# The last output job with tokens standing, and the last LayerNorm done token tile by token tile from PSUM

## The chip, the cores and the metric

The kernel runs on one core of a Trainium2 chip. The metric is the device time of one execution in microseconds (us). TensorE (PE in the rows) does matrix products and transposes into PSUM, VectorE (DVE) and ScalarE (ACT) work on SBUF and PSUM, GpSimd (POOL) works on SBUF, and SyncE (SP) issues the DMAs.

## The reference, cut to what matters

Two models run one behind the other on 512 tokens with 1024 channels. The part that this change touches is the very end of the second: the sum of the residual and the output projection, and the LayerNorm over the channels, whose result is the kernel's output.

```python
def layer_norm(x, g, b):
    xf = x.astype(jnp.float32)
    mu = xf.mean(-1, keepdims=True)
    var = jnp.square(xf - mu).mean(-1, keepdims=True)
    return ((xf - mu) * lax.rsqrt(var + LN_EPS) * g.astype(jnp.float32) + b.astype(jnp.float32)).astype(x.dtype)

def second_block(...):
    ...
        y = jnp.concatenate([y_mix, y_mem], axis=-1) * jax.nn.silu(gate)   # 512 x 2048
        x = layer_norm(ALPHA * x + y @ w_out, pg, pb)                      # w_out: 2048 x 1024
    return x
```

## The kernel before

All products are float32 products of some precision: each operand is split into a high part and a low part (`x_hi`, `x_lo`, `w_hi`, `w_lo`, type fp32r), and three products are summed, hi by hi, hi by lo and lo by hi. The weights come in *jobs* of 256 output columns and 8 blocks of 128 rows. SP loads the weights of a job into `w_raw`, GpSimd splits them (L738 and L751), TensorE multiplies. Two sets of weights and two pairs of PSUM banks (`g_bank` 0 and 1 for even jobs, 2 and 3 for odd ones) are used in turn. A semaphore `w_used` tells that a job's products are done, `g_free` that its banks were read.

Everything but the attention is kept transposed, with channels on the 128 partitions and the 512 tokens in the free dimension: the residual is `hT`, eight chunks of 128 channels by 512 tokens. A job in `products_T` (L888) holds the weights still and moves the tokens: for each of two halves of 128 output channels 8 times 3 matmuls of 512 columns, so 48 in all. Other jobs (`products_nat`, L915) hold a tile of 128 tokens still and move the weights: 24 matmuls of 256 columns for each of the tiles, and the result has tokens on the partitions.

The last projection (`b_out`) is 8 jobs: four with the first half of the 2048 rows, four with the second. After each, VectorE adds the two banks to two chunks of `hT` (L2731 in `add_out`). The last three jobs and the LayerNorm are interleaved, before the change, in `last_output_jobs` on TensorE and in `layer_norm` on VectorE and ScalarE:

- after job 5 TensorE multiplies chunks 0 and 1 by a matrix of ones (L1385), which gives a first estimate of the mean in every partition; VectorE takes it off the chunks (L2774, `centre`), ScalarE squares them (L2070), VectorE sums chunks and squares in PSUM (L2781, `add_up`), all beside jobs 6 and 7;
- after job 7 come the last chunk (L2807, L2774, L2070), the sums over the partitions with the ones (L1395 to L1399), the mean (L1526), the variance (L2822), its transpose to one value per token (L1406), the root (L2077) and the reciprocal (L2828);
- VectorE (L2816) and GpSimd with ScalarE (L856, L1526) take the rest of the mean off and multiply by the gain; TensorE transposes 32 blocks of 128 by 128 to have tokens on the partitions (L1519); VectorE (L2979), or ScalarE and GpSimd (L1526, L869), multiply by the reciprocal root and add the bias row; SP writes eight tiles of 128 by 512 to HBM (L707).

The order of the work is the order of the code on each engine; nothing reorders it. `plan_banks` assigns the four banks of `t_bank` to the transposes and sums in turn. `link` and `done` on VectorE make an instruction signal its own semaphore and make the next one wait for it; `done` also adds one empty instruction for each further semaphore.

## Time and profile before

| what | us |
|---|---|
| median of 3 runs (1693.11 to 1694.98) | 1694.58 |
| the profiled execution's own time | 1694.56 |
| its span in the profile | 1692.8 |
| TensorE busy | 1663.4 (98%) |
| VectorE busy | 916.9 (54%) |
| ScalarE busy | 572.4 (34%) |
| GpSimd busy | 1053.0 (62%) |

The page of the profile lists busy time by engine, the span in 40 slices, the chain of work that ended last, and the costliest groups of instructions. A row of the timeline or of the chain gives start and length in microseconds; `x4` means that four instructions in a row were merged, with the length from the first one's start to the last one's end. The length of a matmul contains its way through the array, so matmuls that follow each other overlap in the rows: the pace is the distance of two starts. TensorE is busy to its last slice but one tenth; in the last of the 40 slices (42 us long) it is busy for 7 tenths.

### The profile page before, as it was taken

The numbers are of one execution on the slowest core, as the hardware profiler recorded it, in microseconds if no ns is written. First come the engines' busy times: TensorE is split into PE (matmuls) and PEld (weight loads), VectorE is DVE, ScalarE is ACT, GpSimd is POOL, SyncE is SP. The second block draws the span as 40 slices with busy tenths as digits, with TensorE's granted clock in tenths as the row PEclk, the third lists the DMA queues.
The fourth block names the chain that finished last, engine by engine and source line by source line (L and its number), as shares of the span: only waits on it lengthen the run. The fifth ranks groups of instructions, "written<-read, shape, count | busy, mean of one in ns | idle before, by whom it ended". The sixth has DMA issues, their size and how long they took to land.

```text
span 1692.8 us, 22289 instructions
## 1 busy us (share of the span) xinstructions
PE 1663.4 (98%) x8073; PEld 1364.6 (81%) x8073; DVE 916.9 (54%) x1411; ACT 572.4 (34%) x990; POOL 1053.0 (62%) x779
## 2 busy tenths in 40 slices
PE   7999999999999999999999999999999999999997
PEld 5897997888878888888888888887878777777785
DVE  5323948782445222221247997998475784443416
ACT  5331248330422100100144445756131345553203
POOL 7676754476647766766774889782577544333563
PEclk9999999999999999999999999999999999999999
DMA  6333333223343323333233332221423321121221
GB/s 207 125 102 121 104 100 125 96 79 100 100 149 94 92 93 95 99 100 100 81 117 101 99 100 90 77 83 54 162 72 106 95 75 51 51 74 51 75 87 50
DMA packets 191274, 162.10 MB, mean 96 GB/s; under 512 B 9684, under 2 KB 187472, under 8 KB 190672
## 3 DMA queue, kind: packets, MB, share of 16 engines
q1 hardware_dynamic: 190984, 160.84, 30.5%
q8 instruction: 56, 0.92, 0.2%
q14 instruction: 34, 0.28, 0.0%
q10 hardware_dynamic: 200, 0.06, 0.0%
HBM read 155.60 MB, written 4.23 MB: 94 GB/s over the span
## 4 chain that ended last, share of the span: by engine, by line
PE 92%; DVE 4%; ACT 2%; POOL 1%; issue 1%; DMA 0%; DVEq 0%; SPq 0%; ACTq 0%
PE g_bank L888 65%; PE g_bank L905 7%; PE g_bank L915 6%; PE t_bank L1465 2%; PE t_bank L1475 2%; PE g_bank L1369 1%; PE t_bank L1205 1%; PE t_bank L1237 1%; PE t_bank L1287 1%; PE t_bank L1308 1%; PE g_bank L1351 1%; PE t_bank L1454 1%; PE t_bank L949 1%; PE t_bank L1445 1%; DVE t_bank L2647 0%
## 5 line engine op out<-in xcount | busy, mean ns | idle before, releaser
L751 POOL TENSOR_TENSOR w_lo<-w_raw,w_hi 128x512 fp32r<-128x512 f32 x392 | 541.1, 1411 | 8.2
L738 POOL TENSOR_SCALAR w_hi<-w_raw 128x2048 fp32r<-128x2048 f32 x98 | 192.6, 1965 | 497.4 <-issue 214.0
L888 PE MATMUL g_bank<-x_hi,w_hi 128*128 128x512 f32 x1248 | 494.8, 396 | 0.2 <-DVEq L2222 0.2
L888 PE MATMUL g_bank<-x_hi,w_lo 128*128 128x512 f32 x1248 | 486.0, 389 | 0.0
L888 PE MATMUL g_bank<-x_lo,w_hi 128*128 128x512 f32 x1248 | 486.0, 389 | 0.0
L888 PEld LDWEIGHTS g_bank<-x_hi,w_hi 128*128 128x128 f32 x1248 | 234.4, 188 | 52.1 <-issue 4.4
L888 PEld LDWEIGHTS g_bank<-x_hi,w_lo 128*128 128x128 f32 x1248 | 234.3, 188 | 49.2
L888 PEld LDWEIGHTS g_bank<-x_lo,w_hi 128*128 128x128 f32 x1248 | 234.5, 188 | 48.5 <-issue 1.7
L2647 DVE SCALAR_TENSOR_TENSOR t_bank<-hc,cols,t_bank 128x512 f32<-128x512 f32 x280 | 187.0, 749 | 4.7 <-DVE hc L2631 2.8
L799 POOL TENSOR_TENSOR w_lo<-w_raw,w_hi 128x512 fp32r<-128x512 f32 x104 | 134.3, 1324 | 68.1 <-ACT w_hi L1868 68.1
L888 PE MATMUL g_bank<-y_hi,w_hi 128*128 128x512 f32 x332 | 130.9, 394 | 0.0
L888 PE MATMUL g_bank<-y_hi,w_lo 128*128 128x512 f32 x332 | 129.4, 390 | 0.0
L888 PE MATMUL g_bank<-y_lo,w_hi 128*128 128x512 f32 x332 | 129.3, 389 | 0.0
L1859 ACT ACTIVATE sg<-gs 128x512 f32<-128x512 f32 x22 | 14.0, 634 | 253.4 <-DVE gs L2598 253.4
L2598 DVE TENSOR_TENSOR gs<-g_bank,rstd 128x512 f32<-128x512 f32 x22 | 15.2, 691 | 139.9 <-PE g_bank L888 139.6
L888 PEld LDWEIGHTS g_bank<-y_hi,w_hi 128*128 128x128 f32 x332 | 62.3, 188 | 14.2 <-issue 0.7
L888 PEld LDWEIGHTS g_bank<-y_hi,w_lo 128*128 128x128 f32 x332 | 62.3, 188 | 13.2
L888 PEld LDWEIGHTS g_bank<-y_lo,w_hi 128*128 128x128 f32 x332 | 62.4, 188 | 12.8 <-issue 0.2
L815 POOL TENSOR_TENSOR pacc<-pacc,prod 128x512 f32<-128x512 f32 x54 | 68.1, 1293 | 0.0
L2907 DVE CUSTOM_DVE_ANT_0 pB<-t_bank,mask 128x128 f32<-128x128 f32 (+3 forms) x48 | 23.6, 491 | 75.1 <-PE t_bank L1465 68.0
L2251 DVE TENSOR_TENSOR hT<-hT,g_bank 128x512 f32<-128x512 f32 x24 | 15.4, 683 | 84.7 <-PE g_bank L888 67.8
L2731 DVE SCALAR_TENSOR_TENSOR hT<-hT,g_bank 128x512 f32<-128x512 f32 x28 | 18.0, 682 | 74.9 <-PE g_bank L888 54.6
(458 smaller groups left out, 2907.3 us busy)
## 6 DMA issues: line engine op xcount, KB each, us to landing
w_raw<-w_gate_up SPq DMA_DIRECT2D x44, 512.0 KB, 5.0
w_raw<-a_w_in SPq DMA_DIRECT2D x44, 512.0 KB, 4.5
w_raw<-b_w_in SPq DMA_DIRECT2D x38, 512.0 KB, 4.3
w_raw<-w_in SPq DMA_DIRECT2D x28, 512.0 KB, 4.8
w_raw<-w_kv SPq DMA_DIRECT2D x16, 512.0 KB, 4.4
w_raw<-w_out_mix SPq DMA_DIRECT2D x16, 512.0 KB, 6.3
w_raw<-w_down SPq DMA_DIRECT2D x16, 512.0 KB, 3.9
w_raw<-a_w_out SPq DMA_DIRECT2D x16, 512.0 KB, 4.0
```

The source lines that it names most:

```text
L738: nc.gpsimd.tensor_scalar(w_hi[:, par], w_raw[:, par], 1.0, 0.0, ALU.mult, ALU.add).then_inc(pool_chain, 1)
L751: last = nc.gpsimd.tensor_tensor(w_lo[:, par, s], w_raw[:, par, s], w_hi[:, par, s].bitcast(F32), ALU.subtract)
L799: last = nc.gpsimd.tensor_tensor(w_lo[:, par, s], w_raw[:, par, s], w_hi[:, par, s].bitcast(F32), ALU.subtract)
L815: nc.gpsimd.tensor_tensor(acc_k[:], acc_k[:], p[:], ALU.add).then_inc(tap_chain, 1)
L888: last = nc.tensor.matmul(g_bank[:, 2 * pair + f, 0:n], ww[:, k0 + k, ws], xk, start=(k == 0 and q == 0), stop=(k == kt - 1 and q == 2))
L905: last = nc.tensor.matmul(g_bank[:, 2 * par + f, :], ww[:, par, k, ws], xx[:, k0 + k, :], start=(k == 0 and q == 0), stop=(k == kt - 1 and ...
L915: last = nc.tensor.matmul(g_bank[:, 2 * par + m // 2, m % 2 * WC:m % 2 * WC + n], xx[:, k, m * P:(m + 1) * P], ww[:, k, 0:n], start=(k == ...
L1465: last = nc.tensor.matmul(b[:, c:c + W_OF[qb]], qB[:, 4 * hg + i, qb * P:(qb + 1) * P], kB[:, 0:W_OF[qb]], start=True, stop=True)
L1475: last = nc.tensor.matmul(b, vB[:, kt, :], pTB[:, pT_at(u) + kt, :], start=(kt == 0), stop=(kt == qb))
L2647: ins = v.scalar_tensor_tensor(tail if k == TAPS - 1 else a(k), h(k), wk, a(k), ALU.mult, ALU.add)
L2731: ins = v.scalar_tensor_tensor(hT[:, k, :], hT[:, k, :], 1.0 if half else ALPHA, g_bank[:, 2 * (j % 2) + f, :], ALU.mult, ALU.add)
L2907: ins = v.tensor_tensor_reduce(p_unit(u, i), b[:, i % per * W_OF[1]:i % per * W_OF[1] + w], mask[:, M_AT[qb]:M_AT[qb] + w], SLOPES[4 * hg ...
```

## The change

The LayerNorm of layer `b` no longer uses the transposed form. `last_output_jobs` and `layer_norm` serve layer `a` only; what they did for layer `b` is replaced:

- TensorE: no product with ones after job 5. Job 6 signals its first half (`w_half`). Then the finished chunks 0 to 3 of `hT` are transposed, 16 blocks, one bank of `t_bank` for each tile of 128 tokens (task `h_out`). Job 7 is computed with tokens standing: for each of the four token tiles two transposes of chunks 4 and 5 into the first half of a bank of `g_bank`, then 24 matmuls of 256 columns into the second half, and between them two matmuls with `ident` that add chunks 6 and 7 into the same accumulation. Bank `H_BANK[m]` then holds the finished residual of channels 512 to 1023 for tile m, bank `h_out` m that of channels 0 to 511; `h_tok` tells it.
- VectorE: for each tile statistics of both banks (`bn_stats`, `bn_aggr`), then (h - mean) * gain for both halves into `onat`, with the reciprocal of the root between them. For the last tile VectorE also multiplies by the reciprocal root and adds the bias.
- ScalarE: the root for each tile, and for tiles 0 to 2 the product with the reciprocal root in place. GpSimd: the bias for tiles 0 to 2.
- SP: one more row of 1024 values is spread over the partitions (`g_row`, the gain), and the eight output tiles are written in the order of the token tiles.

```diff
-            last_output_jobs(JOBS["b_out"], "b", 1)
-            for i in range(8):
-                h, m = i // 4, i % 4
-                pe.wait_ge(fin_dve, (4, GAIN_DVE)[h])
-                if h:
-                    pe.wait_ge(fin_act, DT - GAIN_DVE)
-                b = bank(TASKS["out"] + i)
-                for q in range(4):
-                    last = nc.tensor.transpose(b[:, q * P:(q + 1) * P], hT[:, 4 * h + q, m * P:(m + 1) * P], ident[:])
+            base = JOBS["b_out"]
+            jobs(base + 5, 1, lambda par: products_T(par, x_hi, x_lo))
+            jobs(base + 6, 1, lambda par: products_T(par, x_hi, x_lo, half=w_half))
+            h0 = 48 + 16 + 8
+            for m in range(TT):
+                b = bank(TASKS["h_out"] + m)
+                pe.wait_ge(h_done, h0 + 4)
+                for k in range(4):
+                    last = nc.tensor.transpose(b[:, k * P:(k + 1) * P], hT[:, k, m * P:(m + 1) * P], ident[:])
                 last.then_inc(t_ready, 1)
+            j = base + 7
+            slot(j, j % 2, j // 2)
+            for m in range(TT):
+                ms = slice(m * P, (m + 1) * P)
+                if m == 2:
+                    pe.wait_ge(g_free[(j + 1) % 2], (j + 1) // 2)
+                b = g_bank[:, H_BANK[m], :]
+                for k in range(4, 6):
+                    pe.wait_ge(h_done, h0 + k + 1)
+                    nc.tensor.transpose(b[:, (k - 4) * P:(k - 3) * P], hT[:, k, ms], ident[:])
+                for k in range(KT):
+                    for q, (xx, ww) in enumerate(((x_hi, w_hi), (x_hi, w_lo), (x_lo, w_hi))):
+                        last = nc.tensor.matmul(b[:, WC:2 * WC], xx[:, k, ms], ww[:, j % 2, k, :],
+                                                start=(k == 0 and q == 0), stop=(k == KT - 1 and q == 2))
+                    if k in (0, 1):
+                        nc.tensor.matmul(b[:, WC + k * P:WC + (k + 1) * P], hT[:, 6 + k, ms], ident[:], start=False, stop=False)
+                last.then_inc(h_tok, 1)
...
@@ ScalarE
-            layer_norm("b", 1, True)
-            act.wait_ge(root_tok, 3)
-            for i in OUT_BY_ACT:
...
+            link(nc.scalar.activation(ltok[:, 0, 0:1], eps[:, 1:2], ACT.Sqrt))
+            def token_std(m):
+                act.wait_ge(tok_var, m + 1)
+                nc.scalar.activation(ltok[:, 1, m:m + 1], tvar[:, m, 1:2], ACT.Sqrt, bias=eps[:, 1:2]).then_inc(ln_std, 1)
+            token_std(0)
+            for m in range(TT - 1):
+                act.wait_ge(root_tok, 2 + m + 1)
+                for i in (2 * m, 2 * m + 1):
+                    copy(onat[:, i, :], onat[:, i, :], ltok[:, 2, m:m + 1]).then_inc(on_act, 1)
+                token_std(m + 1)
...
@@ VectorE
-            layer_norm("b", 1, col["b_post_g"], col["b_post_b"], True)
...
+            j = JOBS["b_out"] + 6
+            dve.wait_ge(w_half, 7)
+            v.tensor_tensor(hT[:, 4, :], hT[:, 4, :], g_bank[:, 2 * (j % 2), :], ALU.add).then_inc(h_done, 1)
+            dve.wait_ge(w_used, j + 1)
+            done(v.tensor_tensor(hT[:, 5, :], hT[:, 5, :], g_bank[:, 2 * (j % 2) + 1, :], ALU.add), h_done, g_free[j % 2])
+            dve.wait_ge(in_brow, 32)
+            for m in range(TT):
+                first = ready(TASKS["h_out"] + m)
+                v.bn_stats(out=tstat[:, m, 0, :], in_=first)
+                dve.wait_ge(h_tok, m + 1)
+                both = (first, g_bank[:, H_BANK[m], :])
+                link(v.bn_stats(out=tstat[:, m, 1, :], in_=both[1]))
+                done(v.bn_aggr(out=tvar[:, m, :], in_=tstat[:, m, :, :]), tok_var)
+                for h in range(2):
+                    ins = v.scalar_tensor_tensor(onat[:, 2 * m + h, :], both[h], tvar[:, m, 0:1], g_row[:, h * T:(h + 1) * T],
+                                                 ALU.subtract, ALU.mult)
+                    if h == 0:
+                        link(ins)
+                        dve.wait_ge(ln_std, 1 + m + 1)
+                        link(v.reciprocal(ltok[:, 2, m:m + 1], ltok[:, 1, m:m + 1]))
+                    elif m < TT - 1:
+                        done(ins, root_tok)
+                    else:
+                        link(ins)
+            for h in range(2):
+                i = 2 * (TT - 1) + h
+                v.scalar_tensor_tensor(onat[:, i, :], onat[:, i, :], ltok[:, 2, TT - 1:TT], b_row[:, h * T:(h + 1) * T],
+                                       ALU.mult, ALU.add).then_inc(on_dve, 1)
...
@@ GpSimd
-            less_rest_of_mean(1)
-            pool.wait_ge(in_brow, 16)
-            for n, i in enumerate(OUT_BY_ACT):
...
+            pool.wait_ge(in_brow, 32)
+            for i in range(2 * (TT - 1)):
+                pool.wait_ge(on_act, i + 1)
+                nc.gpsimd.tensor_tensor(onat[:, i, :], onat[:, i, :], b_row[:, i % 2 * T:(i % 2 + 1) * T], ALU.add).then_inc(on_pool, 1)
```

On TensorE, behind the last matmul of job 7, this stood at the end of the program before (each row an instruction with its line, what it writes and reads, and the semaphores it waits for; `ones` and `ident` are constant matrices, `ln_s` and `nring` the sums):

```order
L888 MATMUL g_bank<-x_hi,w_lo 128x512
L1395 MATMUL t_bank<-ln_s,ones 128x512 [waits ln_sums,t_free0,t_free2]
L1395 MATMUL t_bank<-ln_s,ones 128x512 [waits ln_sums]
L1397 MATMUL t_bank<-hT,ones 128x512 [waits ln_cent]
L1399 MATMUL t_bank<-nring,ones 128x512 [waits ln_sq]
L1406 MATMUL t_bank<-ident,rstd 128x128 [waits ln_var,t_free1]
L1406 MATMUL t_bank<-ident,rstd 128x128 x3
L1519 MATMUL t_bank<-ident,hT 128x128 [waits t_free3,fin_dve]
L1519 MATMUL t_bank<-ident,hT 128x128 x3
```

In the changed program this stands on TensorE from the end of job 6 on:

```order
L884 MATMUL g_bank<-x_hi,w_lo 128x512
L1510 MATMUL t_bank<-ident,hT 128x128 [waits h_done,t_free3]
L1510 MATMUL t_bank<-ident,hT 128x128 x3
...
L1521 MATMUL g_bank<-ident,hT 128x128 [waits h_done,g_free1,w_split]
L1521 MATMUL g_bank<-ident,hT 128x128 [waits h_done]
L1524 MATMUL g_bank<-w_hi,x_hi 128x256
L1524 MATMUL g_bank<-w_lo,x_hi 128x256
L1524 MATMUL g_bank<-w_hi,x_lo 128x256
L1527 MATMUL g_bank<-ident,hT 128x128
```

The 32 transposes behind the LayerNorm (L1519) became 16 ahead of job 7 (L1510) and 8 within it (L1521), with 8 products with `ident` (L1527) for the last two chunks; behind the last matmul of job 7 TensorE has nothing left to do, and within job 7 it waits for VectorE only for chunks 4 and 5 and, at tile 2, for the banks of job 6.

On VectorE this stood in the last stretch before (`hg` is the chunk times the gain, `gneg` the gain over -1024, `ltok` values per token):

```order
L2807 SCALAR_TENSOR_TENSOR hT<-hT,g_bank 128x512 [waits dve_chain,w_used]
L2774 SCALAR_TENSOR_TENSOR hT<-t_bank,hT 128x512 [waits dve_chain,t_ready]
L2816 SCALAR_TENSOR_TENSOR hT<-t_bank,gneg,hg 128x512 [waits ln_cent,hg_ready,ln_d,t_ready]
L2822 SCALAR_TENSOR_TENSOR rstd<-t_bank,rstd 128x512 [waits dve_chain,t_ready,ln_dd]
L2816 SCALAR_TENSOR_TENSOR hT<-t_bank,gneg,hg 128x512 [waits dve_chain,hg_ready] x2
L2828 RECIPROCAL ltok<-ltok 128x4 [waits dve_chain,ln_std]
L2816 SCALAR_TENSOR_TENSOR hT<-t_bank,gneg,hg 128x512 [waits dve_chain,hg_ready] x2
L2979 SCALAR_TENSOR_TENSOR onat<-t_bank,ltok,b_row 128x512 [waits dve_chain,ln_d,t_ready,in_brow]
L2979 SCALAR_TENSOR_TENSOR onat<-t_bank,ltok,b_row 128x512 [waits dve_chain,t_ready] x4
```

And this stands there now for the last tile of tokens (the same six rows, L2969 to L2975, stand ahead of it for each of tiles 0 to 2):

```order
L2969 BN_STATS tstat<-t_bank 128x6 [waits dve_chain,t_ready]
L2972 BN_STATS tstat<-g_bank 128x6 [waits h_tok]
L2973 BN_AGGR tvar<-tstat 128x2 [waits dve_chain]
L2975 SCALAR_TENSOR_TENSOR onat<-t_bank,tvar,g_row 128x512 [waits dve_chain]
L2980 RECIPROCAL ltok<-ltok 128x1 [waits ln_std,dve_chain]
L2975 SCALAR_TENSOR_TENSOR onat<-g_bank,tvar,g_row 128x512 [waits dve_chain]
L2987 SCALAR_TENSOR_TENSOR onat<-onat,ltok,b_row 128x512 [waits dve_chain]
L2987 SCALAR_TENSOR_TENSOR onat<-onat,ltok,b_row 128x512
```

What VectorE did for the LayerNorm beside jobs 6 and 7 (L2774, L2781) is gone, and its work of the end hangs on `h_tok`, one tile of tokens at a time.

## Rows read from the trace of the kernel before

**Rows 1.** The chain that ended last: start, length (us), engine, tile, line, count.

```profile
1649.69 1.72 PE t_bank L1385 x4
1651.41 21.81 PE g_bank L888 x96
1673.22 1.72 PE t_bank L1395 x4
...
1676.10 0.61 ACT mean L1526
...
1681.73 4.52 PE t_bank L1519 x24
...
1688.26 0.75 DVE onat L2979
```

**Rows 2.** Busy time by stretch; columns PE, PEld, DVE, ACT, POOL, granted clock, DMA share.

```profile
1662.30:1673.20 10.90, 10.90 (x50) 9.03 (x49) 8.13 (x12) 3.88 (x6) 0.00 (x0) 1.00 0.00 0
1673.20:1681.70 8.50, 4.35 (x13) 1.52 (x11) 5.25 (x8) 3.93 (x7) 3.72 (x3) 1.00 0.00 0
1681.70:1687.20 5.50, 5.38 (x32) 5.14 (x32) 3.00 (x4) 2.20 (x4) 3.40 (x3) 0.69 0.30 110
```

**Rows 3.** Timeline of PE: products with a token tile standing, behind float32 products with `ident`.

```profile
1261.36 1.13 PE L1428 MATMUL t_bank<-ident,ltok 128*128 128x128 f32 x8 [0.45 <-DVEq L2222]
1262.24 0.36 PE L915 MATMUL g_bank<-w_hi,m_hi 128*128 128x256 f32 x1
1262.44 0.28 PE L915 MATMUL g_bank<-w_lo,m_hi 128*128 128x256 f32 x1
...
1267.96 0.28 PE L915 MATMUL g_bank<-w_hi,m_lo 128*128 128x256 f32 x1
```

**Rows 4.** Timeline of PE: four transposes between two products.

```profile
21.43 0.60 PE L974 MATMUL t_bank<-ident,xn_nat 128*128 128x128 f32 x4
21.78 0.48 PE L1055 MATMUL g_bank<-x_hi,w_hi 128*128 128x512 f32 x1
22.09 0.39 PE L1055 MATMUL g_bank<-x_lo,w_hi 128*128 128x512 f32 x1
```

**Rows 5.** Timeline of DVE: statistics of a row of 1024, from SBUF.

```profile
330.65 1.42 DVE L2497 BATCH_NORM_STATS2 mstat<-mem 128x6 f32<-128x512 f32 x2 [0.24 <-DVE hT L2421]
332.10 0.21 DVE L2498 BATCH_NORM_AGGREGATE mstat<-mstat 128x2 f32<-128x12 f32 x1
```

**Rows 6.** Timeline of DVE in the last LayerNorm.

```profile
1673.26 0.69 DVE L2807 SCALAR_TENSOR_TENSOR hT<-hT,g_bank 128x512 f32<-128x512 f32 x1 [0.75 <-PE g_bank L888]
...
1679.64 0.75 DVE L2816 SCALAR_TENSOR_TENSOR hT<-t_bank,gneg,hg 128x512 f32<-128x512 f32 x1 [0.16 <-DVE hT L2816]
1680.54 0.18 DVE L2828 RECIPROCAL ltok<-ltok 128x4 f32<-128x4 f32 x1
```

**Rows 7.** Timeline of DVE and of POOL around the split of job 7's weights.

```profile
1651.85 2.48 DVE L2774 SCALAR_TENSOR_TENSOR hT<-t_bank,hT 128x512 f32<-128x512 f32 x4
...
1654.44 1.80 DVE L2781 TENSOR_TENSOR t_bank<-hT 128x512 f32<-128x512 f32 x1
...
1658.83 0.70 DVE L2781 TENSOR_TENSOR t_bank<-t_bank,hT 128x512 f32<-128x512 f32 x1 [0.89 <-ACT nring L2070]
...
1651.87 5.51 POOL L751 TENSOR_TENSOR w_lo<-w_raw,w_hi 128x512 fp32r<-128x512 f32 x4
```

**Rows 8.** Groups by line of the last 98 us: count, busy us, mean ns, idle before.

```profile
L869 POOL TENSOR_TENSOR onat<-onat,b_row 128x512 f32<-128x512 f32 x3 | 3.8, 1268 | 3.3 <-ACTq L2204 3.3
...
L1526 ACT ACTIVATE onat<-t_bank,ltok 128x512 f32<-128x512 f32 x3 | 2.1, 687 | 2.2 <-PE t_bank L1519 2.2
```

**Rows 9.** DMA issues of the end: the last output tile, the bias row (us to landing last).

```profile
1689.19 0.33 SPq L707 DMA_DIRECT2D out<-onat  x1
...
L700 SPq DMA_DIRECT2D b_row<-b_post_b x1: 351/351/351, 1636.5 to 1636.5; - x1
...
b_row<-b_post_b SPq DMA_DIRECT2D x1, 512.0 KB, 5.8
```

More of the change, by code:

```diff
@@ L144 @@
     + [(f"idx{g}", 4) for g in range(4)] + mem_late_tasks(1, 0) + [("idx4", 4)] + [t for n in range(N_SLOTS) for t in slot_tasks(n)]
-    + [("ln_b", 4), ("out", 8)])
+    + [("h_out", TT)])
 def taps_after():
@@ L698, in _ @@
             stream(JOBS["b_out"] + 4, 4, w_cols("b_w_out_2", 0, 4))
-            sp.wait_ge(t_ready, TASKS["ln_b"])
-            sp.dma_start(b_row[:], A["b_post_b_2"][0].partition_broadcast(P)).then_inc(in_brow, 16)
-            for i in range(8):
-                h, m = i // 4, i % 4
-                if i in OUT_BY_ACT:
-                    sp.wait_ge(on_pool, OUT_BY_ACT.index(i) + 1)
-                else:
-                    sp.wait_ge(on_dve, sum(q not in OUT_BY_ACT for q in range(i + 1)))
-                sp.dma_start(out[0, m * P:(m + 1) * P, h * T:(h + 1) * T], onat[:, i, :]).then_inc(out_done[i % 2], 16)
+            sp.wait_ge(t_ready, TASKS["h_out"])
+            for row, src in ((g_row, "b_post_g_2"), (b_row, "b_post_b_2")):
+                sp.dma_start(row[:], A[src][0].partition_broadcast(P)).then_inc(in_brow, 16)
+            for m in range(TT):
+                for h in range(2):
+                    if m < TT - 1:
+                        sp.wait_ge(on_pool, 2 * m + h + 1)
+                    else:
+                        sp.wait_ge(on_dve, h + 1)
+                    sp.dma_start(out[0, m * P:(m + 1) * P, h * T:(h + 1) * T], onat[:, 2 * m + h, :]).then_inc(out_done[h], 16)
             for done_sem in out_done:
@@ L851, in _ @@
             nc.gpsimd.iota(dist_i[:], pattern=[[-1, T]], base=T - P, channel_multiplier=1).then_inc(dist_ready, 1)
-            def less_rest_of_mean(layer):
-                pool.wait_ge(ln_d, layer + 1)
-                for k in range((LESS_DVE, GAIN_DVE)[layer], DT):
-                    nc.gpsimd.tensor_tensor(hT[:, k, :], hT[:, k, :], mean[:], ALU.subtract).then_inc(ln_pool, 1)
-            less_rest_of_mean(0)
+            pool.wait_ge(ln_d, 1)
+            for k in range(LESS_DVE, DT):
+                nc.gpsimd.tensor_tensor(hT[:, k, :], hT[:, k, :], mean[:], ALU.subtract).then_inc(ln_pool, 1)
             job(odd, 0, 32 * (odd // 2) + 48, odd - 1)
@@ L2765, in _, with layer_norm @@
                     out_weights_lo(3)
-            def layer_norm(name, layer, gain, bias, last_norm):
+            def layer_norm(name, layer, gain, bias):
                 ln, base = TASKS[f"ln_{name}"], JOBS[f"{name}_out"]
@@ L2823, in layer_norm @@
                      t_free[BANK[ln + 2]], ln_var)
-                if last_norm:
-                    for k in range(GAIN_DVE):
-                        if k == 3:
-                            dve.wait_ge(ln_std, layer + 1)
-                            done(v.reciprocal(ltok[:, 2, :], ltok[:, 1, :]), root_tok)
-                        if k >= 1:
-                            less_d(k, d)
-                    dve.wait_ge(ln_d, layer + 1)
-                    dve.nop().then_inc(t_free[BANK[ln + 1]], 1)
-                    return
                 for k in range(LESS_DVE):
@@ L2973, in _ @@
             add_out(JOBS["b_out"], 0, 6)
-            layer_norm("b", 1, col["b_post_g"], col["b_post_b"], True)
-            dve.wait_ge(in_brow, 16)
-            for i in range(8):
-                if i not in OUT_BY_ACT:
-                    r = TASKS["out"] + i
-                    done(v.scalar_tensor_tensor(onat[:, i, :], ready(r), ltok[:, 2, i % 4:i % 4 + 1],
-                                                b_row[:, i // 4 * T:(i // 4 + 1) * T], ALU.mult, ALU.add), t_free[BANK[r]], on_dve)
+            j = JOBS["b_out"] + 6
[4 more added lines that the diff above has]
+            dve.wait_ge(in_brow, 32)
+            for m in range(TT):
+                first = ready(TASKS["h_out"] + m)
[13 more added lines that the diff above has]
+                        done(ins, root_tok)
+                    else:
+                        link(ins)
+            for h in range(2):
+                i = 2 * (TT - 1) + h
+                v.scalar_tensor_tensor(onat[:, i, :], onat[:, i, :], ltok[:, 2, TT - 1:TT], b_row[:, h * T:(h + 1) * T],
+                                       ALU.mult, ALU.add).then_inc(on_dve, 1)
 _NAMES = ["x", "mem", "mix_norm", "w_in", "conv_w", "conv_b", "dt_bias", "a_log", "d_skip", "ssd_norm", "pool_w",
```

51 lines of the change are left out of this document (11 added, 40 removed).

## The prediction

> **What bounds the kernel now.** I read the page first: TensorE is busy for 98% of the span, so only what shortens its stream, or the part behind its stream, can count. Then the chain of waits in order of time [rows 1]. It runs through the products without a gap until 1673.22, and from there through a serial tail: sums with ones, ScalarE's mean, VectorE's steps, transposes, VectorE's last output tile. The last VectorE step ends at 1688.26 + 0.75 = 1689.01, and the span at 1692.8. So 1673.22 to 1689.01, 15.8 us, is the part in which TensorE waits for other engines or does small things for them, and the last 3.8 us are the output's way to HBM. Last the busy times by stretch [rows 2]: in 1673.2 to 1681.7 no engine is busy for more than 5.25 of 8.5 us. The tail is a chain, not a throughput limit; the change can win there at most those 15.8 us less what it needs itself.
>
> **Part 1, TensorE until the end of job 6.** The two products with ones after job 5 (1.72 us of the chain [rows 1]) go. Job 6 ran 10.9 us, as job 7 did [rows 2]; from 1649.69 it now ends at 1660.6, not 1662.3. What VectorE did beside jobs 6 and 7 (8 to 9 us in each) goes too, at no gain: TensorE did not wait for it.
>
> **Part 2, sixteen transposes** ahead of job 7. Four transposes stand between two products in 21.78 - 21.43 = 0.35 us [rows 4], 0.088 each, so 1.4 us: job 7 starts at 1662.0. They need chunks 0 to 3, which VectorE finished right after job 5, near 1651. Behind them chunk 5 is wanted: VectorE starts it 0.04 us after job 6 (as it did after job 7, 1673.26 against 1673.22 [rows 6, 1]) and needs 0.69 and a signal, so it is there at 1661.5. The transposes cover it with 0.5 us to spare; without the cover TensorE would wait those 0.9 us itself.
>
> **Part 3, job 7 with tokens standing.** Before: 48 matmuls of 512 columns, 10.9 us. Now 96 of 256 columns. In the rows of such a job 46 starts lie between 1262.44 and 1267.96: 0.120 each [rows 3], so 24 take 2.88 us. For each tile come two transposes (0.18, and 0.08 for the longer first product behind them: 22.09 - 21.78 = 0.31 against 0.227 for a product of 512 columns, 10.9 / 48), and two float32 products with `ident`: such products appear as two records each, 8 records took 1262.24 - 1261.36 = 0.88 us, 0.22 a product, and the product behind took 0.20 instead of 0.12 [rows 3]; so 2 x (0.22 + 0.08) = 0.60. A tile is 2.88 + 0.26 + 0.60 = 3.74 us, four are 15.0. That is 4.1 us more than job 7 took: 0.6 since 96 at 0.120 take longer than 48 at 0.227, and 4 x 0.86 for the transposes and `ident` products. Lower end: no switching costs, 3.50 a tile. Upper end: every switch costs as much as a whole 512-column product (0.227) in place of 0.08, 3.74 + 3 x 0.15 = 4.2 a tile. I take 3.74, since both forms have rows of their own. The tiles end at 1665.7, 1669.5, 1673.2 and 1677.0.
>
> **Part 4, VectorE for each tile.** `bn_stats` of 512 from SBUF: two with the wait between them in 1.42, so 0.69 each; `bn_aggr` 0.21 [rows 5]. From PSUM it is not in the trace; VectorE's 512-column operations there take 0.69 to 0.75 [rows 6], which bounds it narrowly: I take 0.69. The scalar_tensor_tensor from PSUM with a value per partition and a row from SBUF takes 0.75 (L2816, L2979 [rows 6, 1]); the reciprocal 0.18, here of one column, 0.17. Busy per tile 2 x 0.69 + 0.21 + 2 x 0.75 + 0.17 = 3.26. The gaps: 0.03 to 0.04 where only its own semaphore is waited for (332.10 - 330.65 - 1.42 [rows 5]), 0.15 where a signal or a second wait stands between (1680.54 - 1679.64 - 0.75 [rows 6]). Six gaps are 0.2 at the least and 0.9 at the most; three of the kind with a signal (behind `bn_aggr`, ahead of the reciprocal, at the end of the tile) and three plain ones make 0.57. A tile takes VectorE 3.83 us (3.45 to 4.2), TensorE 3.74: the two are even, and VectorE is late by a hair. It starts the second half's statistics of tile 0 at 1665.7 + 0.04 and of tile 3 at 1665.75 + 3 x 3.83 = 1677.25; TensorE would allow 1677.0. The root on ScalarE, of one column, lies beside the first scalar_tensor_tensor of 0.75.
>
> **Part 5, behind the last tile.** Statistics 0.69, aggregate 0.21, 0.75, 0.17, 0.75, then two more scalar_tensor_tensor at 0.75: 4.07, with gaps of 0.04, 0.15, 0.15, 0.04, 0.04 and 0.03 it is 4.5 (4.2 to 4.9). VectorE ends at 1681.8. From there to the span's end it was 3.8 us [rows 1]; the last tile was issued at 1689.19 [rows 9], and I keep 3.8. The outputs now leave two in each 3.8 us instead of eight in the last 5, so the last of them finds the DMA engines free; that may give up to half a microsecond that I don't count.
>
> **Part 6, beside the path.** ScalarE multiplies tiles 0 to 2 (0.69 each), GpSimd adds the bias (1.27 each [rows 8]), six times now instead of three: 1.4 and 2.5 us a tile, under 3.8. For tile 2 VectorE signals at about 1676.4, ScalarE's first product is there at 1677.2, GpSimd is through at 1679.8, ahead of VectorE's own last tile (1681.8), for which SP waits last. The DMA of the gain row stands on SP ahead of that of the bias, which was issued at 1636.5 and landed 5.8 us later [rows 9]; two of them are there before 1649, and VectorE first asks at 1661.5. The weights of job 7 were split by 1657.4 [rows 7], ahead of the 1660.6 at which job 7 could now want them, and behind the transposes 1662.0.
>
> **The sum.** VectorE's end moves from 1689.0 to 1681.8, so 7.2 us go: minus 15.8 (the old tail) minus 1.7 (ones) plus 1.4 (transposes) plus 4.1 (job 7) plus 0.3 (VectorE behind TensorE) plus 4.5 (the new tail). Against the profiled execution's own 1694.56, which is the median of the runs (1694.58) to 0.02, that gives 1687.4.
>
> **The rivals.**
> (a) *The tile costs more than its parts*, on VectorE by gaps (4.2 us a tile and 4.9 behind: 1665.75 + 12.6 + 4.9 = 1683.3) or on TensorE by switches (4.2 a tile: 1662.0 + 16.8 + 4.5 = 1683.3): both give 1.5 us more, 1688.9. For it: no row shows float32 products in the midst of an fp32r sum, nor VectorE in this rhythm. Against it: every part has a row.
> (b) *GpSimd and VectorE get in each other's way in the last stretch.* The rows show what it costs: with both inputs in SBUF and GpSimd at work VectorE's sum took 1.80 us, with one input in PSUM and GpSimd idle 0.70; with one input in PSUM and GpSimd busy it was not slowed, four in 2.48 [rows 7]. The last two operations (L2987) have both inputs in SBUF. By my times GpSimd ends at 1679.8 and they start at 1680.2, a margin of 0.4 us. If it is late, one or both take 1.8: plus 1.1 to 2.1, so 1688.5 to 1689.5.
> The Trainium skill says the same in "SBUF — State Buffer", section "Who interferes with whom": a VectorE instruction with two SBUF inputs contends with a GpSimd instruction that reads SBUF, the other blocks fully, and one SBUF input is free of it. By that rule, the trace agrees: 1.80 us against 0.70.
> (c) *TensorE's granted clock falls in the token block: slower than before.* The granted clock was 1.00 through all jobs, and 0.69 on average in 1681.7 to 1687.2, after 8.5 us in which TensorE was busy for only 4.35 [rows 2]; the transposes then took 4.52 / 24 = 0.188 each instead of 0.088 [rows 1, 4]. If it fell at the transposes and stayed down, the block from 1660.6 to 1677.0 would run at half speed (1.2 in place of 2.4 GHz), up to 16.4 us more: 1703.8. It is slower than before as soon as more than 7.2 us of the block's work is done at the low level. Against it: there is no idle time between its instructions, and the products behind float32 products with `ident` kept their pace of 0.120 [rows 3], as did those behind transposes [rows 4].
> (d) *The change hardly does what it says*: the new tail is as long as the old. It would need 3.8 us more than (a), or all of (a), (b) and a short spell of low clock (3.4 us): about 1691 to 1692. Nothing speaks for it alone.
>
> **How the numbers follow.** Forecast 0.60; (a) 0.20; (b) 0.10; (c) 0.03; (d) 0.05; better than forecast by over 1.5 us 0.02. The likeliest is 1687.4. Its ends: without switching costs and with the shortest gaps the tile is TensorE's 3.5 and the tail 4.2, 1.3 us less, and half a microsecond on the way out, so 1685.5; upwards (a) and (b) one on the other, 1691. The range takes (a) or (b), and a little of both: 1685.4 to 1690.2. What a measurement of this kernel can tell from no change is 0.2%, 3.4 us: faster means below 1691.2. Forecast, (a) and (b) are faster, (d) is half within: faster 0.92, same 0.05, slower 0.03.
>
> **What would show it.** Job 7 as four blocks of 3.7 us ending near 1677; VectorE's tiles at 3.8 us with no idle time of more than 0.2 us ahead of the second statistics; each L2987 at 0.75; VectorE's end near 1681.8, the span near 1685.6; granted clock 1.00 until 1677. Wrong it would be by a tile of over 4.2 us on either engine, L2987 above 1 us, statistics from PSUM above 0.8, or a granted clock of 0.5 before the last matmul.

## The result, and where the time went

| what | before | after |
|---|---|---|
| median of the runs, us | 1694.68 (1693.11 to 1694.98, 4 runs) | 1684.74 (1683.73 to 1684.9, 4 runs) |
| ratio, 95% interval | | 0.9941 [0.9929, 0.9953] |
| profiled execution, its span | 1694.56, 1692.8 | 1684.83, 1683.0 |
| VectorE's last output step ends | 1689.01 | 1680.52 |
| from there to the span's end | 3.8 | 2.5 |
| TensorE busy | 1663.4 (98%) | 1657.1 (98%) |

The change makes the kernel 0.59% faster (0.47 to 0.71%), 9.9 us. The forecast was 7.2 us and 1687.4; the measured median lies 0.7 us below the lower end of the range, 1685.4, and so in the outcome "better than forecast by over 1.5 us", to which the prediction gave a chance of 0.02. Against the profiled execution the miss is 1687.4 - 1684.83 = 2.6 us. The mechanism came as forecast, one chain in place of another; several of its terms were too large, above all the outputs' way to HBM.

The chain of waits after, which answers to [rows 1] (start and length in us, engine, tile, line, count). The new program's lines: L884 `products_T`; L1510 the sixteen transposes; L1521, L1524 and L1527 the transposes, products and `ident` products of job 7; L2969 and L2972 the statistics of the two halves; L2975 and L2987 the scalar_tensor_tensor ahead of and behind the reciprocal root.

```profile
1638.40 21.77 PE g_bank L884 x96
1660.17 1.75 PE t_bank L1510 x16
1661.91 0.22 PE g_bank L1521 x2
1662.13 0.36 PE g_bank L1524 x3
1662.49 0.22 PE g_bank L1527 x2
...
1663.30 2.16 PE g_bank L1524 x18
...
1665.48 0.71 DVE tstat L2972
...
1679.10 0.75 DVE onat L2987
1679.86 0.66 DVEq L216
```

TensorE is the chain up to the first tile of job 7, and from 1665.48 on it is VectorE to the end: this is the "VectorE is late by a hair" of Part 4. A tile is 3.57 us of TensorE's chain here (1661.91 to 1665.48), not 3.74.

The timeline of VectorE after, for the first tile, the start of the second, and the last, answers to [rows 5, 6] (start, length, engine, line, operation, out and in; in brackets the idle time before and what ended it):

```profile
1665.48 0.70 DVE L2972 BATCH_NORM_STATS2 tstat<-g_bank 128x6 f32<-128x512 f32 x1 [3.57 <-PE g_bank L1524]
1666.21 0.21 DVE L2973 BATCH_NORM_AGGREGATE tvar<-tstat 128x2 f32<-128x12 f32 x1
1666.59 0.75 DVE L2975 SCALAR_TENSOR_TENSOR onat<-t_bank,tvar,g_row 128x512 f32<-128x512 f32 x1 [0.16 <-DVE tvar L2973]
1667.37 0.16 DVE L2980 RECIPROCAL ltok<-ltok 128x1 f32<-128x1 f32 x1
1667.57 0.75 DVE L2975 SCALAR_TENSOR_TENSOR onat<-g_bank,tvar,g_row 128x512 f32<-128x512 f32 x1
1668.48 0.70 DVE L2969 BATCH_NORM_STATS2 tstat<-t_bank 128x6 f32<-128x512 f32 x1 [0.15 <-DVE onat L2975]
1669.09 0.68 DVE L2972 BATCH_NORM_STATS2 tstat<-g_bank 128x6 f32<-128x512 f32 x1
...
1676.26 0.68 DVE L2972 BATCH_NORM_STATS2 tstat<-g_bank 128x6 f32<-128x512 f32 x1
...
1679.10 1.42 DVE L2987 SCALAR_TENSOR_TENSOR onat<-onat,ltok,b_row 128x512 f32<-128x512 f32 x2
```

Statistics from PSUM take 0.70, against 0.69 worked out for SBUF. Between tile 0 and tile 3 VectorE's second statistics are (1676.26 - 1665.48) / 3 = 3.59 us apart. Both L2987 together take 1.42: nothing slows them. The last of GpSimd's work, beside it:

```profile
1676.38 2.49 POOL L865 TENSOR_TENSOR onat<-onat,b_row 128x512 f32<-128x512 f32 x2 [1.04 <-ACT onat L1534]
```

It ends at 1678.87, 0.23 us before L2987 begins. Busy times by stretch after, against [rows 2] (PE, PEld, DVE, ACT, POOL, granted clock, DMA share, GB/s):

```profile
1660.60:1662.30 1.70, 1.70 (x18) 1.70 (x16) 0.99 (x2) 0.00 (x0) 0.00 (x0) 1.00 0.00 0
1663.00:1675.00 12.00, 12.00 (x104) 12.00 (x103) 8.43 (x17) 3.56 (x7) 4.73 (x4) 1.00 0.13 46
1675.00:1680.00 5.00, 1.03 (x9) 0.82 (x7) 4.55 (x9) 1.63 (x3) 2.82 (x3) 1.00 0.46 175
1680.00:1683.00 3.00, 0.00 (x0) 0.00 (x0) 0.52 (x1) 0.00 (x0) 0.00 (x0) 0.50 0.61 227
```

The granted clock stays at 1.00 through the transposes and job 7 and falls only when TensorE has nothing left to do. At last the output's way: the tile view of `out`, before (first two lines) and after (last two).

```profile
L707 SPq DMA_DIRECT2D out<-onat x8: 332/396/464, 1684.7 to 1689.2; - x8
DMA to landing us min/median/max: 2.1/2.7/3.3
```

```profile
L708 SPq DMA_DIRECT2D out<-onat x8: 332/332/344, 1670.6 to 1680.5; - x8
DMA to landing us min/median/max: 2.0/2.0/3.9
```

Eight outputs of 256 KB left within 4.5 us before and needed 2.7 us each in the median; now they leave over 10 us and need 2.0. The same view, narrowed to the last output of the kernel before, gives 3.2 for it:

```profile
L707 SPq DMA_DIRECT2D out<-onat x1: 332/332/332, 1689.2 to 1689.2; - x1
DMA to landing us min/median/max: 3.2/3.2/3.2
```

So the 3.8 us of before are 0.2 from VectorE's end to the issue, 3.2 to the landing and 0.4 from there to the span's end. The 2.5 us of after are 0.03 (VectorE ends at 1680.52, the row below is SP's issue), 2.0 and 0.4.

```profile
1680.55 0.33 SPq L708 DMA_DIRECT2D out<-onat  x1
```

### The profile page after: what moved, and what is told of

Read it like the earlier page. It is cut to its first block, busy times and chain, and to the rows that moved or that the text cites. A ratio compares the mean times of both kernels' runs of the same rounds, so it can differ in the third digit from the quotient of the medians.

```text
span 1683.0 us, 22297 instructions
## 1 busy us (share of the span) xinstructions
PE 1657.1 (98%) x8113; PEld 1364.3 (81%) x8113; DVE 904.8 (54%) x1402; ACT 564.4 (34%) x978; POOL 1052.7 (63%) x779
## 4 chain that ended last, share of the span: by engine, by line
PE 92%; DVE 4%; ACT 2%; issue 1%; POOL 1%; DMA 0%; DVEq 0%; SPq 0%; ACTq 0%
PE g_bank L884 65%; PE g_bank L901 7%; PE g_bank L911 6%; PE t_bank L1466 2%; PE t_bank L1456 2%; PE g_bank L1365 1%; PE t_bank L1201 1%; PE t_bank L1233 1%; PE t_bank L1283 1%; PE t_bank L1304 1%; PE g_bank L1051 1%; PE g_bank L1347 1%; PE t_bank L1445 1%; PE t_bank L945 1%; PE t_bank L1436 1%
## 5 line engine op out<-in xcount | busy, mean ns | idle before, releaser
L884 PE MATMUL g_bank<-x_hi,w_hi 128*128 128x512 f32 x1232 | 488.3, 396 | 0.1
L884 PE MATMUL g_bank<-x_hi,w_lo 128*128 128x512 f32 x1232 | 479.9, 390 | 0.0
L884 PE MATMUL g_bank<-x_lo,w_hi 128*128 128x512 f32 x1232 | 479.8, 389 | 0.0
L884 PEld LDWEIGHTS g_bank<-x_hi,w_hi 128*128 128x128 f32 x1232 | 231.5, 188 | 51.1 <-issue 4.2
L884 PEld LDWEIGHTS g_bank<-x_hi,w_lo 128*128 128x128 f32 x1232 | 231.3, 188 | 48.5
L884 PEld LDWEIGHTS g_bank<-x_lo,w_hi 128*128 128x128 f32 x1232 | 231.5, 188 | 47.8 <-issue 1.4
L884 PE MATMUL g_bank<-y_hi,w_hi 128*128 128x512 f32 x332 | 130.9, 394 | 0.0
L884 PE MATMUL g_bank<-y_hi,w_lo 128*128 128x512 f32 x332 | 129.4, 390 | 0.0
L884 PE MATMUL g_bank<-y_lo,w_hi 128*128 128x512 f32 x332 | 129.3, 389 | 0.0
L884 PEld LDWEIGHTS g_bank<-y_hi,w_hi 128*128 128x128 f32 x332 | 62.4, 188 | 14.2 <-issue 0.7
L884 PEld LDWEIGHTS g_bank<-y_hi,w_lo 128*128 128x128 f32 x332 | 62.3, 188 | 13.1
L884 PEld LDWEIGHTS g_bank<-y_lo,w_hi 128*128 128x128 f32 x332 | 62.4, 188 | 12.8 <-issue 0.2
L777 POOL TENSOR_TENSOR kv_lo<-w_raw,kv_hi 128x512 fp32r<-128x512 f32 x32 | 41.1, 1319 | 27.7 <-ACT kv_hi L1640 27.7
```

Of the source, the lines that this page charges most:

```text
L777: last = nc.gpsimd.tensor_tensor(lo[:, s], raw_w[:, s], hi[:, s].bitcast(F32), ALU.subtract)
L884: last = nc.tensor.matmul(g_bank[:, 2 * pair + f, 0:n], ww[:, k0 + k, ws], xk, start=(k == 0 and q == 0), stop=(k == kt - 1 and q == 2))
```

## The experiments

The stretch up to the end of job 6 is the same code in `after` and in all its variants, and it still ends at different times: 1660.17 in the profiled execution of `after`, 1659.08, 1660.54, 1659.02 and 1660.37 in four variants. Executions differ by 1.5 us before the place that is changed, so a difference of 0.3 us between two executions tells nothing. So I compare spans from the end of job 6 on (`after`: 1683.0 - 1660.17 = 22.8), or rows within the end, and times only for large effects.

**1. The kernel before, with only its last two outputs written.** To see whether the 3.8 us are a fixed way or a queue.

```diff
-                sp.dma_start(out[...], onat[:, i, :]).then_inc(out_done[i % 2], 16)
+                if i >= 6:
+                    sp.dma_start(out[...], onat[:, i, :]).then_inc(out_done[i % 2], 16)
             for done_sem in out_done:
-                sp.wait_ge(done_sem, 16 * 4)
+                sp.wait_ge(done_sem, 16)
```

> The kernel before, but only the last two of the eight output tiles (128 x 512 each) are written to HBM; the other six stay unwritten. Theory Q (queue): before, the outputs left eight in 5 us and the DMA engines moved them one behind the other, so the last one landed 3.2 us after its issue; with two alone it lands after 2.0 to 2.2, and from VectorE's last step to the span's end it is 2.6 to 2.8 us in place of 3.8. Rival F (fixed): those 3.8 us are the price of the signal, the issue and one transfer in this form of code (an empty instruction carries the signal), whatever stands ahead in the queue; then they stay 3.7 to 3.8. VectorE's last step itself ends at the same 1689 (+-1) in both.

Measured: 1692.36 (one run), span 1690.6. The tile view of `out` and VectorE's last step:

```profile
L708 SPq DMA_DIRECT2D out<-onat x2: 343/352/361, 1687.3 to 1688.2; - x2
DMA to landing us min/median/max: 2.0/2.0/2.0
```

```profile
1687.25 0.75 DVE L2980 SCALAR_TENSOR_TENSOR onat<-t_bank,ltok,b_row 128x512 f32<-128x512 f32 x1 [0.24 <-DVE onat L2980]
```

VectorE ends at 1688.00 and the span 2.6 us later, not 3.8. Nothing but the six outputs and the waits for them was taken out: outputs ahead in the queue cost the last one 1.2 us. Theory Q holds, F falls.

**2. The changed kernel, with all outputs held back until the last tile.** The same question the other way round.

```diff
+            sp.wait_ge(on_dve, 1)
             for m in range(TT):
                 for h in range(2):
```

> The changed kernel, but SP issues no output tile before VectorE has finished the first half of the last tile of tokens, so all eight tiles leave at the end. Theory Q: 2.1 MB at some 380 GB/s are 5.5 us from about 1680.7 on, so the span ends near 1686.6 to 1687.2 in place of 1683.0, 3.6 to 4.2 us later, time 1688.3 to 1688.9, and the last tile lands 3 us or more after its issue. Rival F: the last tile lands 2.0 us behind its issue all the same; only SP's own issues (eight at about 0.6) push it, at most 1.5 us.

Measured: 1687.96 (1687.75 to 1688.89, 5 runs), ratio to before 0.9964 [0.995, 0.9978]; 3.2 us more than the changed kernel.

```profile
1675.33 0.68 DVE L2973 BATCH_NORM_STATS2 tstat<-g_bank 128x6 f32<-128x512 f32 x1
...
1678.18 1.42 DVE L2988 SCALAR_TENSOR_TENSOR onat<-onat,ltok,b_row 128x512 f32<-128x512 f32 x2
```

```profile
L709 SPq DMA_DIRECT2D out<-onat x8: 343/502/652, 1679.0 to 1682.8; - x8
DMA to landing us min/median/max: 2.0/2.8/3.0
```

VectorE ends at 1679.60, the span at 1686.2, 6.6 us later against 2.5. Two parts make the 4.1 us more: the last issue comes at 1682.8, 3.2 us behind VectorE in place of 0.03, and its landing takes 3.0 in place of 2.0. The issues of the burst are long themselves, 0.50 us in the median, and the last three are 0.69 us apart (1681.4 to 1682.8). At the 380 GB/s of the expectation 256 KB take just as long, so SP issues them at the pace at which the outputs move; whether the full queue holds it back no run here separates. Theory Q holds for the sum: 4.1 us lies in its 3.6 to 4.2. F falls, as the landing is 3.0 and the issues cost more than its 1.5. The time is below Q's 1688.3, since job 6 had ended 0.9 us earlier in this execution (1659.25 against 1660.17).

**3. The changed kernel without the overlap.** VectorE waits for all four tiles ahead of its first second-half statistics.

```diff
-                dve.wait_ge(h_tok, m + 1)
+                dve.wait_ge(h_tok, TT)
```

> The changed kernel, but VectorE waits for all four tiles of job 7 before it takes the second half's statistics of the first; every instruction stays. Theory O (overlap): the gain comes from three of four tiles' VectorE work lying beside job 7. Then VectorE starts at 1676.1 and ends at 1676.1 + 3 x 3.58 + 4.26 = 1691.1, the span at 1693.6, time 1695.3: 10.6 us more than the changed kernel, level with the kernel before within 0.1%. Rival W (less work): the gain comes from fewer and shorter steps of the LayerNorm, and the order matters little; then this is at most 3.6 us (one tile) behind the changed kernel, time below 1688.5.

Measured: 1695.2 (1693.87 to 1695.59, 10 runs), ratio to before 1.0004 [0.9995, 1.0014].

```profile
1676.25 0.70 DVE L2972 BATCH_NORM_STATS2 tstat<-g_bank 128x6 f32<-128x512 f32 x1 [14.15 <-PE g_bank L1524]
...
1679.86 0.68 DVE L2972 BATCH_NORM_STATS2 tstat<-g_bank 128x6 f32<-128x512 f32 x1
...
1689.87 1.42 DVE L2987 SCALAR_TENSOR_TENSOR onat<-onat,ltok,b_row 128x512 f32<-128x512 f32 x2
```

The whole gain is gone, to within 0.1%: theory O holds, W falls, and without the overlap of VectorE's tiles with job 7 nothing is won. The LayerNorm in this form is not shorter in itself. From the end of job 5 (1649.69 before, here job 6 ended at 1660.35, so 1649.45) to VectorE's end it took 39.3 us before and takes 41.8 here (1691.29), 2.5 more; the shorter way out, 2.5 us here too, gives 1.3 of it back. VectorE needs 3.6 us a tile here too (1676.25 to 1679.86), with TensorE idle, so that pace is its own.

**4. Who sets the pace of the tiles.** The changed kernel with the transposes of chunks 4 and 5 ahead of job 7 and without the `ident` products.

```diff
-                for k in range(4, 6):
-                    pe.wait_ge(h_done, h0 + k + 1)
-                    nc.tensor.transpose(b[:, (k - 4) * P:(k - 3) * P], hT[:, k, ms], ident[:])
+                pe.wait_ge(h_done, h0 + 6)
+                if m == 0:
+                    ... (all eight transposes, for the four banks)
...
-                    if k in (0, 1):
-                        nc.tensor.matmul(b[:, WC + k * P:WC + (k + 1) * P], hT[:, 6 + k, ms], ident[:], start=False, stop=False)
```

> The changed kernel, with the eight transposes of chunks 4 and 5 moved ahead of job 7 and the eight products with ident left out (channels 768 to 1023 of the residual are missing from the sum). Job 7 is then 96 plain products of 256 columns: 24 x 0.120 = 2.9 us a tile instead of the 3.53 measured. Theory V (VectorE sets the pace of the end, 3.58 us a tile from tile 0 on): tile 0 is finished at about 1665.7, 0.2 later than in the changed kernel, VectorE's second statistics still follow each other by 3.58, the last ones start at about 1676.5, and the time is the same or 0.2 to 0.3 us longer, about 1685.0. Theory T (TensorE sets the pace, as it is busy without a gap until the last tile): the last statistics start at 1665.7 + 3 x 2.9 = 1674.4 and the time is 1.9 us shorter, about 1682.8.

Measured: 1684.9 (1683.89 to 1685.4, 4 runs), ratio to before 0.9944 [0.9929, 0.996]. The chain of waits:

```profile
1659.08 1.75 PE t_bank L1510 x16
1660.83 0.87 PE g_bank L1525 x8
1661.70 2.89 PE g_bank L1528 x24
```

and VectorE's second statistics of tiles 0 and 3:

```profile
1664.61 0.70 DVE L2974 BATCH_NORM_STATS2 tstat<-g_bank 128x6 f32<-128x512 f32 x1 [3.79 <-PE g_bank L1528]
...
1675.39 0.68 DVE L2974 BATCH_NORM_STATS2 tstat<-g_bank 128x6 f32<-128x512 f32 x1
```

TensorE's tile is 2.89 us, and VectorE's statistics are still (1675.39 - 1664.61) / 3 = 3.59 apart. From the end of job 6 to the span's end it is 1682.2 - 1659.08 = 23.1, 0.3 more than in the changed kernel: tile 0 came later by the six transposes of the other tiles less its own two `ident` products (two records each, so 2 x 0.109), and all the rest behind it. Theory V holds, T falls: 3 x 0.65 = 2 us taken from TensorE gave nothing. So within this end VectorE's own 3.59 us a tile is the limit, not TensorE's 3.53.

**5. VectorE's share lightened.** The changed kernel, with the four first-half statistics ahead of the wait for tile 0.

```diff
             for m in range(TT):
-                first = ready(TASKS["h_out"] + m)
-                v.bn_stats(out=tstat[:, m, 0, :], in_=first)
+                v.bn_stats(out=tstat[:, m, 0, :], in_=ready(TASKS["h_out"] + m))
+            for m in range(TT):
+                first = t_bank[:, BANK[TASKS["h_out"] + m], :]
```

> The changed kernel, with VectorE's four first-half statistics (0.70 us each) ahead of the wait for tile 0 instead of one at the head of each tile. VectorE's own work on a tile falls from 3.58 to about 2.9 us, and TensorE's 3.53 sets the pace. Theory V (VectorE is late by 0.05 us a tile): the second statistics follow each other by 3.53, with 0.6 us of idle time ahead of each, the last ones start 0.15 to 0.3 us earlier than in the changed kernel (about 1676.0 to 1676.1), and the time falls by those 0.2 to 0.3 us, about 1684.5, less than three rounds can tell. If instead VectorE were the only thing in the way, the time would fall by 3 x 0.65 = 2 us, to about 1682.8.

Measured: 1684.86 (1684.54 to 1685.4, 4 runs), ratio to before 0.9943 [0.9928, 0.9959].

```profile
1665.86 0.70 DVE L2973 BATCH_NORM_STATS2 tstat<-g_bank 128x6 f32<-128x512 f32 x1 [1.78 <-PE g_bank L1524]
...
1669.39 0.70 DVE L2973 BATCH_NORM_STATS2 tstat<-g_bank 128x6 f32<-128x512 f32 x1 [0.69 <-PE g_bank L1524]
...
1676.44 0.70 DVE L2973 BATCH_NORM_STATS2 tstat<-g_bank 128x6 f32<-128x512 f32 x1 [0.69 <-PE g_bank L1524]
```

Now TensorE ends VectorE's wait at every tile, after 0.7 us of idle time on VectorE, and the statistics are 3.53 us apart. The last statistics begin 1676.44 - 1660.54 = 15.9 us behind job 6, against 1676.26 - 1660.17 = 16.1. The two engines' paces are 3.59 and 3.53, and lifting the one brings only the difference. The median, 1684.86 against 1684.74, does not show it, as was expected of so small a gain.

**6. The price of GpSimd beside L2987, rival (b).** The changed kernel, with two further GpSimd sums into a scratch tile behind its last one.

```diff
+            for i in range(2):
+                nc.gpsimd.tensor_tensor(ln_s[:, i, :], b_row[:, 0:T], b_row[:, T:2 * T], ALU.add)
```

> The changed kernel, and GpSimd makes two more sums of 512 columns from SBUF into a tile that nobody reads, right behind its last bias sum (which ended at 1678.9), so it is busy until about 1681.4, beside VectorE's two L2987 operations (both inputs in SBUF, 0.75 each, from 1679.1). Rival (b) of the prediction: each of these two is held up while GpSimd works, 1.3 to 1.8 us each, and the span grows by 1.1 to 2.1 us. Its counter-theory: three-operand operations with a value per partition don't suffer as the plain sum (1.80) did; they stay at 0.75 and the span at 1683.0 (+-0.3).

Measured: 1685.61 (one run), span 1683.9. VectorE's last two steps, and the added sums:

```profile
1678.21 3.20 DVE L2989 SCALAR_TENSOR_TENSOR onat<-onat,ltok,b_row 128x512 f32<-128x512 f32 x2
```

```profile
1677.93 2.93 POOL L867 TENSOR_TENSOR ln_s<-b_row 128x512 f32<-128x512 f32 x2
```

3.20 us instead of 1.42: the collision costs 1.8 us, within the 1.1 to 2.1 given for it. The span ends 24.6 us behind job 6 (1659.28), 1.8 more than in the changed kernel. In the changed kernel it does not happen, since GpSimd is 0.23 us ahead.

By the Trainium skill ("SBUF — State Buffer", "Who interferes with whom") a VectorE instruction with two SBUF inputs contends with a GpSimd instruction that reads SBUF; the trace agrees, 3.20 against 1.42 us.

**7. A shorter last output.** As number 5, and the last half tile is scaled and written in two pieces of 256 columns. Of the edit only VectorE's part is shown; SP issues the two pieces one by one.

```diff
-            for h in range(2):
+            for h, a, e in ((0, 0, T), (1, 0, T // 2), (1, T // 2, T)):
                 i = 2 * (TT - 1) + h
-                v.scalar_tensor_tensor(onat[:, i, :], ...)
+                v.scalar_tensor_tensor(onat[:, i, a:e], ...)
```

> As the kernel with the early statistics, and VectorE's last output half tile is scaled and written in two pieces of 256 columns (128 KB each) instead of one of 512. Theory Q (the way out is queue plus one transfer, about 2.5 us with a free queue): the early statistics give 0.2 to 0.3 us; the last piece is issued 0.1 us later for one more VectorE instruction and lands sooner, since it is half as large: 0.2 to 0.4 us less, about 1684.2 in all. Theory F (a fixed time of 2 us for each output transfer, whatever its size): only the early statistics count, less the extra instruction, 1684.6.

Measured: 1683.5 (1683.32 to 1685.16, 5 runs), ratio to before 0.9939 [0.9925, 0.9952]. That looks like 1.2 us less than the changed kernel, but the intervals of the ratios overlap almost wholly, and in the profiled execution job 6 had already ended 1.15 us earlier. From there:

```profile
1659.02 1.75 PE t_bank L1510 x16
```

```profile
1677.78 1.54 DVE L2988 SCALAR_TENSOR_TENSOR onat<-onat,ltok,b_row 128x512 f32<-128x512 f32 x3
```

VectorE ends at 1679.32, 20.30 behind job 6 (20.35 in the changed kernel), the span at 1681.8, 2.5 later. The last piece of 128 KB lands 1.9 us after its issue, where 256 KB took 2.0; at 380 GB/s the smaller size alone would be worth an estimated 0.3. It is issued 0.09 us behind VectorE's end in place of 0.03, so the way out stays 2.5. The early statistics give 0.2, the further instruction takes 0.13. Theory Q's saving by size is not there, and F holds to 0.1 us, for outputs that follow each other by 0.4 us; a piece that stands alone was not tried. The time itself fell below both theories (1684.2 and 1684.6), and in the profiled execution the 1.15 us in front of the change account for that. No version here is shown to be faster than the changed kernel.

The Trainium skill ("DMA: Bandwidth & Descriptors", "Anatomy of one DMA — SWDGE (gpsimd) path") puts a fixed 2.0 us and, besides, the bytes over 436 GB/s on each transfer, for transfers that GpSimd issues. By its figures an estimate would be 2.6 us for 256 KB and 2.3 for 128 KB. The trace does not agree for outputs that SP issues: the whole landing of each of the two outputs of 256 KB in number 1 took 2.0, bytes included, and the measurement decides.

**8. The transposes twice.** The changed kernel, with each of the sixteen done two times.

```diff
-                for k in range(4):
+                for k in (0, 1, 2, 3, 0, 1, 2, 3):
```

> The changed kernel, with each of the sixteen transposes ahead of job 7 done twice, 32 in a row. Theory P (the pace of a float32 transpose in a long row is 0.109 us, as 16 in 1.75 show, and there was no cost of starting): 32 take 3.5 us, the end moves by 1.75 us, to about 1686.5. Theory S (each is 0.088 us, as predicted from four between two products, and the other 0.35 us are a cost of the switch or a wait that comes once): 32 take 1.75 + 1.4 = 3.15 us, about 1686.1.

Measured: 1686.71 (one run), span 1685.0.

```profile
1660.37 3.50 PE t_bank L1510 x32
```

3.50 / 32 = 0.109 us each, as 1.75 / 16. From the end of job 6 to the span's end it is 24.6, 1.8 more. Theory P holds: this is the pace of a float32 transpose in a row, and nothing comes once.

## Why the prediction missed, and which terms were off

The 2.6 us of the miss, from the forecast's own places in the profile (positive: the forecast was too late):

| place | forecast | measured | miss |
|---|---|---|---|
| end of job 6 | 1660.6 | 1660.17 | +0.4 |
| sixteen transposes | 1.4 | 1.75 | -0.35 |
| job 7's start to the statistics of tile 0 | 3.74 | 3.57 | +0.2 |
| three tiles on VectorE | 11.5 | 10.78 | +0.7 |
| statistics of tile 3 to VectorE's end | 4.55 | 4.26 | +0.3 |
| way out | 3.8 | 2.48 | +1.3 |

**The way out (Part 5) is the step that failed**, and half of the miss. I carried 3.8 us over from before and wrote "that may give up to half a microsecond that I don't count". It gave 1.3. The sign and the reason were there; the size was not worked out, though the trace of before had it. There the eight outputs, 2.1 MB, were issued within 4.5 us, and the DMA engines had no pause. This is their busy share in tenths and their rate in the kernel before, in 40 slices of 0.42 us from 1676 to 1693:

```profile
DMA  0000000000000000000000499999979999970000
GB/s 0 0 0 0 0 0 0 0 0 0 0 0 0 0 0 0 0 0 0 0 0 0 164 386 362 400 386 366 376 275 390 371 386 390 386 280 24 14 0 0
```

From 1685.4 to 1691.2 they ran at up to 400 GB/s, 2 us longer than outputs were issued. The last output waited for the ones ahead: its landing took 3.2 us, while 2.1 was the smallest of the same eight. With a free queue the same rows give 0.2 to the issue, 2.1 to the landing and 0.4 to the span's end, 2.7 us, so 1.1 of the 1.3 could have been forecast. The rest is the issue, 0.03 us behind VectorE's end in place of 0.18: before, an empty instruction carried VectorE's signal to SP (`done`), now its last step signals itself; no run tests this part alone. Experiments 1 and 2 show the queue from both sides, 2.6 us in the kernel before with two outputs and 6.6 in the changed kernel with eight at once.

**Tiles on VectorE (Part 4).** The durations were right, 3.25 busy against 3.26. The gaps were not: 0.57 forecast, 0.34 measured (0.03, 0.17, 0.03, 0.04 and 0.16 along the rows above, less 0.09 by which the second statistics begin before the first end). The wait for ScalarE's root, which I priced as a signal of 0.15, cost 0.03, since the root had come during the 0.75 before it. A wait that is long met cost no more here than the engine's wait for itself; 0.15 to 0.17 stands only behind the aggregate and at the end of the tile, the two places where `done` puts an empty instruction in between. At 3.59 in place of 3.83 three tiles are the 0.7 us; the same shorter gaps, and the overlap of the two L2987, make the 0.3 of the tail.

**Tiles on TensorE (Part 3).** 3.53 to 3.57 instead of 3.74. The timeline of TensorE after, around the first pair of records of an `ident` product, answers to [rows 3]:

```profile
1662.21 0.28 PE L1524 MATMUL g_bank<-w_hi,x_lo 128*128 128x256 f32 x1
1662.33 0.39 PE L1527 MATMUL g_bank<-ident,hT 128*128 128x128 f32 x2
1662.47 0.36 PE L1524 MATMUL g_bank<-w_hi,x_hi 128*128 128x256 f32 x1
1662.67 0.28 PE L1524 MATMUL g_bank<-w_lo,x_hi 128*128 128x256 f32 x1
```

The longer first product that I forecast is there, 0.20 us to the next start in place of 0.12. The pair ahead of it takes only 0.14, where I had 0.22 from a row of eight records that began behind idle time. So a pair costs 0.14 + 0.08 = 0.22 in all, not 0.30: 0.109 for a record. Six records at 0.109 and 24 products at 0.120 make 3.54. Why the eight records of [rows 3] took longer, 0.96 with their 0.08, no run here tells. In Part 2 I left the 0.08 out instead, and had 0.088 for 0.109 a transpose. [Rows 4] say 0.108 if read from the first transpose to the second product behind: (22.09 - 21.43 - 0.227) / 4. That these misses have opposite signs is luck.

**The end of job 6** is 0.4 us early against the forecast. The chain is 0.5 us ahead long before the change: a run of products that starts at 340.15 in the kernel before starts at 339.66 after. Jobs 5 and 6 took 21.77 us in the chain, 10.9 each, as forecast. The code ahead of it ran in 1.5 us of spread from one execution to another, so I give these 0.4 us no cause; that they went the way they did is luck.

**What came as said.** The two engines' paces are even and VectorE is late by a hair: 3.59 against 3.53, shown by taking 2 us off TensorE for nothing (number 4) and by making it wait for TensorE with its own load lighter (number 5). The transposes cover chunk 5, which was there at 1660.9 while they ran until 1661.9. Statistics from PSUM cost what they cost from SBUF. Part 1's and Part 6's covers hold.

**The rivals.** (a) The tile cost less than its parts, not more. (b) has its mechanism and price confirmed (number 6), and its condition not met: the margin was 0.23 us where I had 0.4. By number 6 a lost margin would have cost up to 1.8 us. (c) The granted clock was 1.00 until TensorE's last product. (d) falls with the result; number 3 shows what it would have taken: without the overlap the new end is as long as the old. The prediction's figures for (d) do not fit each other: 3.8 us more than (a) is 1692.7, not 1691 to 1692, and an end as long as the old would have meant 1694.6. Nothing else in it hangs on them.

**The range** ended at 1685.4 since I let the lower side have only gaps and switches at their least, and half a microsecond of the queue. Its sum was also off: tiles of 3.5 on TensorE put the statistics of tile 3 at 1662.0 + 14.0 + 0.04 = 1676.0, and a tail of 4.2 puts VectorE's end at 1680.2, 1.6 us before 1681.8 and not 1.3. With these 1.6 and the 1.1 of the way out that the rows bore out, the lower end would have been 1684.7, about what was measured.

## What to carry to other kernels

When outputs that left in a burst come to leave one by one, price the last transfer by the smallest landing in the old trace, not by the last, and add the time to its issue and the time from its landing to the end. Where two engines run in step on tiles, work out both paces before taking work off either: the gain is only the distance to the other. And count a foreign instruction within a stream from the start before it to the second instruction behind it, or its cost is lost or counted twice.
